# First norm's sums on VectorE, input first, and one weight tile behind every second modulation unit

## The reference, cut to what matters

```python
h = x + pos_embed_2d(rows, GRID_W, D)[None]          # latent tokens
hc = ctx                                             # context tokens
ml = (silu(c) @ w_ada + b_ada).reshape(B, 9, D)      # modulation, latent
mc = (silu(c_ctx) @ w_ada + b_ada).reshape(1, 9, D)  # modulation, context
u  = modulate(rmsnorm(h,  norm_g[0]), ml[:, 0], ml[:, 1])
uc = modulate(rmsnorm(hc, norm_g[0]), mc[:, 0], mc[:, 1])
h  = h  + 0.5 * ml[:, 2] * swiglu(u,  ffn_w_in[0], ffn_w_out[0])
hc = hc + 0.5 * mc[:, 2] * swiglu(uc, ffn_w_in[0], ffn_w_out[0])
```

## Time and profile before

| what | us |
|---|---|
| median of 3 runs | 2897.46 (2894.49 to 2897.83) |
| profiled execution | 2883.62 |
| its span, first to last instruction | 2881.8 |
| PE busy in it | 2823.4 (98%) |
| DVE busy | 1633.4 (57%) |
| ACT busy | 968.0 (34%) |
| POOL busy | 237.2 (8%) |

### The profile page before, as it was taken

The page is one execution under the profiler, slowest core; times in us unless marked ns, Lnnn a source line. Parts: engine busy times, 40 slices in busy tenths (PEclk is TensorE's granted clock), DMA queues, the critical chain, the costliest instruction groups (busy, mean ns, idle before and its releaser), DMA issues. The chain is left out here.

```text
span 2881.8 us, 47633 instructions
## 1 busy us (share of the span) xinstructions
PE 2823.4 (98%) x17840; PEld 2475.6 (86%) x17840; DVE 1633.4 (57%) x2197; ACT 968.0 (34%) x1443; POOL 237.2 (8%) x388
## 2 busy tenths in 40 slices
PE   5999999999999999999999999999999999999998
PEld 3688888888888888888888888878999999999998
DVE  2557677676776652223225666655675555555555
ACT  2222222222222221121214555544354444444444
POOL 3000000000000000000101013555120000000001
PEclk8999999999999999999999999999999999999999
DMA  9766676667888856555563566695556556566664
GB/s 361 282 215 209 203 225 202 220 214 232 316 303 317 296 198 203 195 191 165 193 194 105 164 183 194 197 271 167 157 176 193 188 188 189 182 189 189 189 189 147
DMA packets 410321, 604.42 MB, mean 210 GB/s; under 512 B 52960, under 2 KB 303840, under 8 KB 401520
## 3 DMA queue, kind: packets, MB, share of 16 engines
q1 hardware_dynamic: 361536, 417.42, 46.0%
q10 hardware_dynamic: 48688, 185.73, 19.4%
HBM read 560.02 MB, written 43.02 MB: 209 GB/s over the span
## 5 line engine op out<-in xcount | busy, mean ns | idle before, releaser
L1943 DVE TENSOR_TENSOR wl<-raw,wh 128x1024 fp32r<-128x1024 f32 x638 | 782.0, 1232 | 833.8 <-ACT wh L1467 832.0
L1467 ACT CAST wh<-raw 128x1024 fp32r<-128x1024 f32 x638 | 664.6, 1047 | 1466.9 <-PE ps L760 1426.0
L759 PE MATMUL ps<-xl,wh 128*128 128x512 f32 (+1 forms) x2560 | 968.8, 378 | 0.0
L758 PE MATMUL ps<-xh,wh 128*128 128x512 f32 (+1 forms) x1904 | 722.3, 379 | 3.2 <-DVE xl L1994 2.5
L760 PE MATMUL ps<-xh,wl 128*128 128x512 f32 (+1 forms) x1904 | 716.7, 376 | 0.0
L759 PEld LDWEIGHTS ps<-xl,wh 128*128 128x128 f32 x2560 | 481.9, 188 | 89.2
L758 PEld LDWEIGHTS ps<-xh,wh 128*128 128x128 f32 x1904 | 358.7, 188 | 77.7 <-issue 8.4
L760 PEld LDWEIGHTS ps<-xh,wl 128*128 128x128 f32 x1904 | 358.2, 188 | 65.9
L758 PE MATMUL ps<-x2h,wh 128*128 128x256 f32 x1408 | 394.8, 280 | 1.7 <-DVE x2l L1994 1.7
L759 PE MATMUL ps<-x2l,wh 128*128 128x256 f32 x1408 | 396.0, 281 | 0.0
L760 PE MATMUL ps<-x2h,wl 128*128 128x256 f32 x1408 | 394.6, 280 | 0.0
(11 more groups left out here) (274 smaller groups left out, 2665.9 us busy)
## 6 DMA issues: line engine op xcount, KB each, us to landing
raw<-in_ffn_w_in SPq DMA_DIRECT2D x704, 256.0 KB, 3.5
raw<-in_ffn_w_out SPq DMA_DIRECT2D x176, 512.0 KB, 4.5
abuf<-in_w_ada ACTq DMA_DIRECT2D x64, 1024.0 KB, 6.7
abuf<-in_w_ada ACTq DMA_DIRECT2D x96, 512.0 KB, 3.9
xl<-d_h ACTq DMA_DIRECT2D x80, 512.0 KB, 4.3
ada_t<-in_ada SPq DMA_DIRECT2D x64, 512.0 KB, 9.1
raw<-in_w_in SPq DMA_DIRECT2D x128, 256.0 KB, 3.5
raw<-in_w_out SPq DMA_DIRECT2D x32, 512.0 KB, 4.9
```

The source lines that it names most:

```text
L758: mm(out, ah, bh, start=first, stop=False, skip_group_check=reopened)
L759: mm(out, ah, bl, start=False, stop=False, skip_group_check=reopened)
L1467: nc.scalar.copy(wh[:, t % HL, :], raw[:, t % RAW, :]).then_inc(hi_done, 1)
L1943: tt(tl, raw[:, t % RAW, :], th.bitcast(F32), ALU.subtract).then_inc(lo_done, 1)
```

## The change

- SP requests the two halves of the latent input first, ahead of all of `w_ada` (they were issued by ACT, between its other loads). The context halves stay on ACT.
- SP requests a weight tile behind every second unit (i = 1, 3, ..., 15: tiles 0 to 7) instead of one behind each unit from i = 3 on (tiles 0 to 12).
- The position table and the 13 additions of squares move from POOL to DVE. POOL keeps the power -0.5.
- PE's `norm` stands in unit i = 2 (the third unit) instead of i = 4.
- PE works tile t behind unit 2t + 3: tiles 0 to 5 behind units 3, 5, 7, 9, 11, 13 instead of 6, 7, 8, 9, 11, 13.
- DVE norms one feature block per unit, and splits tile t behind unit 2t + 2, the unit just ahead of the tile's own. ACT rounds tile t behind blocks 2t and 2t + 1. Tiles 7 and 8 are split ahead of the last columns, tile 9 behind the last block.

```diff
-FIRST_TILES = {6: 0, 7: 1, 8: 2, 9: 3, 11: 4, 13: 5, 15: 6}
+FIRST_TILES = {2 * t + 3: t for t in range(K_TILES - 1)}
...
+            for b in range(2):
+                k = slice(8 * b, 8 * b + 8)
+                sp.dma_start(h_lat[:, k, :], xT[:, k, :]).then_inc(x_in[b], 16)
             for i in range(ADA_SS):
                 ada_load(i)
-                if i >= 3:
-                    up_load(0, 0, i - 3)
-            for x in range(ADA_SS - 3, UP_TILES):
+                if i % 2:
+                    up_load(0, 0, i // 2)
+            for x in range(K_TILES, UP_TILES):
                 up_load(0, 0, x)
...
-                    if i == 4:
+                    if i == 2:
                         norm(0, NTOK, 7)
...
-            for t in range(AHEAD):
+            for t in range(K_TILES - 1):
+                high(0, 2 * t)
+                high(0, 2 * t + 1)
                 split(0, 0, t)
...
+            def position(b):
+                rows, wide = SEQ // GRID_W, GRID_W
+                dve.wait_ge(x_in[b], 16)
...
+                tt(lat, lat, add.broadcast_to([P, 8, rows, wide]), ALU.add).then_inc(h_set, 1)
+
+            def add_squares(k):
+                dve.wait_ge(sq_done, squares_at(0, k))
+                if k == 1:
+                    i = tt(nacc[:], sq[:, 0, :], sq[:, 1, :], ALU.add)
+                else:
+                    dve.wait_ge(nacc_done, sums_at(0, k) - 1)
+                    i = tt(nacc[:], nacc[:], sq[:, k % 2, :], ALU.add)
+                i.then_inc(nacc_done, 1)
...
             start()
-            k = 0
-            for i in range(ADA_SS):
+            for b in range(2):
+                position(b)
+            for k in range(1, 10):
+                add_squares(k)
+            ada_row(0, 4)
+            for k in range(10, KT - 2):
+                add_squares(k)
+            first_columns(0)
+            ada_row(1, 5)
+            mean_square(0, NTOK, 7)
+            ada_row(2, 4)
+            first_columns(1)
+            dve.wait_ge(cols_set, 2)
+            for k in range(2):
+                scaled(0, k, 7)
+            for k in range(2):
+                low(0, k)
+            split(0, 0, 0)
+            for i in range(3, ADA_SS):
                 ada_row(i, 4 + i % 2)
-                if i:
-                    first_columns(i - 1)
-                if i == 3:
-                    for t in range(AHEAD):
-                        split(0, 0, t)
-                if i == 4:
-                    mean_square(0, NTOK, 7)
-                if i >= 5:
-                    dve.wait_ge(cols_set, i)
-                    now = range(k, min(2 * (i - 4), i))
-                    for k in now:
-                        scaled(0, k, 7)
-                    for k in now:
-                        low(0, k)
-                    k += 1
-                if i in FIRST_TILES:
-                    split(0, 0, FIRST_TILES[i] + AHEAD)
+                first_columns(i - 1)
+                dve.wait_ge(cols_set, i)
+                scaled(0, i - 1, 7)
+                low(0, i - 1)
+                if i % 2 == 0:
+                    split(0, 0, i // 2 - 1)
+            split(0, 0, K_TILES - 1)
+            split(0, 0, K_TILES)
             first_columns(ADA_SS - 1)
             dve.wait_ge(cols_set, ADA_SS)
-            for k in range(k, KT):
-                scaled(0, k, 7)
-                low(0, k)
+            scaled(0, KT - 1, 7)
+            low(0, KT - 1)
+            split(0, 0, K_TILES + 1)
             up_pairs(0, 0)
```

More of the change, by code:

```diff
@@ L1472, in start @@
                     k = slice(8 * b, 8 * b + 8)
-                    act.dma_start(h_lat[:, k, :], xT[:, k, :]).then_inc(x_in[b], 16)
                     act.dma_start(h_ctx[:, k, :], ctxT[:, k, :]).then_inc(x_in[2 + b], 16)
@@ L1518, in load_piece, with up_pairs @@
                     act.dma_start(abuf[:, i % 2].rearrange("p s n -> p (s n)"), src).then_inc(abuf_in[i % 2], 16)
-            def up_pairs(r, m, before=None):
+            def up_pairs(r, m):
                 for x in range(UP_TILES):
-                    if before is not None:
-                        before(x)
-                    split(r, UP_TILES, m * UP_TILES + x + AHEAD)
+                    if m or x >= K_TILES - 1:
+                        split(r, UP_TILES, m * UP_TILES + x + AHEAD)
                     if x < LOAD_AT and m:
@@ L1853, in _ @@
                 square(0, k, 2)
-            for t in range(AHEAD):
+            for t in range(K_TILES - 1):
+                high(0, 2 * t)
+                high(0, 2 * t + 1)
                 split(0, 0, t)
[L1857 to L1862, removed]
+            high(0, KT - 2)
+            split(0, 0, K_TILES - 1)
+            split(0, 0, K_TILES)
+            high(0, KT - 1)
+            split(0, 0, K_TILES + 1)
+            up_pairs(0, 0)
             with act.Fori(0, PIECE_BOTH - 1) as r:
@@ L1952, in start @@
                 dve.wait_ge(cpad_set, 3)
+            def position(b):
+                rows, wide = SEQ // GRID_W, GRID_W
+                dve.wait_ge(x_in[b], 16)
+                lat = h_lat[:, 8 * b:8 * b + 8, :].rearrange("p k (r c) -> p k r c", c=wide)
+                if b == 0:
+                    add = cols[:, C_POSR:C_POSC].rearrange("p (k r) -> p k r", r=rows).unsqueeze(3)
+                else:
+                    add = cols[:, C_POSC:C_IDENT].rearrange("p (k c) -> p k c", c=wide).unsqueeze(2)
+                tt(lat, lat, add.broadcast_to([P, 8, rows, wide]), ALU.add).then_inc(h_set, 1)
[3 more added lines that the diff above has]
+                    i = tt(nacc[:], sq[:, 0, :], sq[:, 1, :], ALU.add)
+                else:
+                    dve.wait_ge(nacc_done, sums_at(0, k) - 1)
+                    i = tt(nacc[:], nacc[:], sq[:, k % 2, :], ALU.add)
+                i.then_inc(nacc_done, 1)
             def ada_row(i, bank):
@@ L2516, in _ @@
             start()
-            k = 0
-            for i in range(ADA_SS):
-                ada_row(i, 4 + i % 2)
-                if i:
-                    first_columns(i - 1)
-                if i == 3:
-                    for t in range(AHEAD):
-                        split(0, 0, t)
-                if i == 4:
-                    mean_square(0, NTOK, 7)
-                if i >= 5:
-                    dve.wait_ge(cols_set, i)
-                    now = range(k, min(2 * (i - 4), i))
-                    for k in now:
-                        scaled(0, k, 7)
-                    for k in now:
-                        low(0, k)
-                    k += 1
-                if i in FIRST_TILES:
-                    split(0, 0, FIRST_TILES[i] + AHEAD)
+            for b in range(2):
[17 more added lines that the diff above has]
+            for i in range(3, ADA_SS):
+                ada_row(i, 4 + i % 2)
+                first_columns(i - 1)
[4 more added lines that the diff above has]
+                    split(0, 0, i // 2 - 1)
+            split(0, 0, K_TILES - 1)
+            split(0, 0, K_TILES)
             first_columns(ADA_SS - 1)
             dve.wait_ge(cols_set, ADA_SS)
-            for k in range(k, KT):
-                scaled(0, k, 7)
-                low(0, k)
+            scaled(0, KT - 1, 7)
+            low(0, KT - 1)
+            split(0, 0, K_TILES + 1)
             up_pairs(0, 0)
@@ L2722, in _ @@
             pool.wait_ge(half_set, 1)
[L2723 to L2733, removed]
+            pool.wait_ge(ms_done, 2)
+            rms(slice(0, NTOK // P))
             norm_streams()
```

## The result

The changed kernel takes 2901.39 us (median of 12 runs, 2890.45 to 2906.11) against 2894.54 us of the kernel before (12 runs, 2884.16 to 2897.83). The ratio is 1.0028, 95% interval 1.0015 to 1.0041: some 8 us slower, and clear of no change, since the interval leaves out 1. The forecast was 2 us faster.

What follows compares the result with a forecast made beforehand. PE bounds the kernel through the end of its first stage. The norm's 15.6 us gain, less 13.6 given back in waits for splits, leaves 2.0: 2897.46 - 2.0 = 2895.5 us, range 2882 to 2902.

Steps and rivals of the forecast that it cites:

- What bounds the kernel: Whole kernel: PE is busy from 137 us to 1000 us, so the time it gets through the first stage decides.
- all of a shift of the first stage reaches the end: Behind the first evacuation by ACT: whatever is gained or lost ahead of it is kept to the end.
- The norm earlier by 15.6: Norm behind the third unit: its spreading ends at 41.85 us instead of 57.45, 15.6 us earlier.
- The branch with the high level: PE at the norm: high clock shortens quarter, columns, sums and spreading by 3.0 us; gain 5.0, 2892.5 us; chance 20%.
- The work moved to DVE hidden: Position table and 13 additions on DVE, ahead of the norm: cost nothing, with a cover of 0.8 to 8.6 us.
- The new wait: Ahead of each tile: split ready 5.02 us behind the unit's copy, PE ready at 2.9, so PE waits some 2.1 us.
- The chain's 12.73 us per cycle: Tile loop: PE copy, DVE, ACT, DVE, PE set the cycle of two units and a tile, 5.02 + 7.71 us.
- The weight tiles requested later: SP's requests: five tiles fewer ahead of the last quarter, 6.5 us of DMA, taking nothing off PE.
- the step that a tile behind this wait takes 5.7 us: Tile loop: a tile was counted as 5.6 us of PE's own work, with the clock staying high.
- The third rival: Tile loop: the clock falls in seven waits of 2.1 us; 17 us slower, 2914.5 us; chance 8%.
- The rival's price of 19 for seven falls: Tile loop: each clock fall loses 2.8 us, 19 in all, less the gain of 2.0, so 17 slower.
- The chances: Whole kernel: faster by over 0.2% 27%, slower by over 0.2% 11%, within 62%; low clock at norm, chain-bound loop 59%.

Runs made afterwards that it cites:

- the filler of 16: The changed kernel with 16 useless matmuls on PE ahead of each of tiles 0 to 5; ratio 1.0088 to the kernel before.
- the last experiment: The changed kernel with each tile split one unit earlier and PE waiting for x block by block within a tile; ratio 0.9959 to the kernel before.
- the short filler: The changed kernel with 5 useless matmuls on PE ahead of each of tiles 0 to 5; ratio 0.9995 to the kernel before.
- mean first: The kernel before, with DVE splitting tiles 0, 1 and 2 behind the norm's mean instead of behind unit 3; ratio 0.9993 to the kernel before.
- split between scaled and low: The changed kernel, ACT rounding tile t behind block 2t (t > 0), DVE splitting it ahead of block 2t + 1's low part; ratio 0.9965 to the kernel before.

## Why the prediction was wrong

What bounds the kernel, and that all of a shift of the first stage reaches the end: right. Before and after agree behind the evacuation within 0.7 us.

The norm earlier by 15.6: right, 15.4. The quarters came as counted, and the level at the norm was the low one in this execution. The branch with the high level exists too, in two of the eight traces with the new order (the filler of 16 and the last experiment, from 37.27 and 37.21 us): there the spreading began 2.7 us earlier than in the changed kernel (3.0 was worked out).

The work moved to DVE hidden: right. The table took 2.29 a half and an addition 0.69, by the duration of single instructions, which is near the lower bound.

The new wait, 2.1 us per tile: right, 2.23 by its rows. The chain's 12.73 us per cycle: right where the clock stood, 12.74 in the experiment with the short filler and 12.75 with the input on ACT. That it fits to the hundredth is luck: in the trace with the short filler it was 5.10 us from the copy to the tile and not 5.02 (68.58 to 73.68), and 7.64 from the tile to the next copy and not 7.71 (60.94 to 68.58).

The weight tiles requested later cost nothing: right; PE waits for no quarter in the loop.

Wrong was the step that a tile behind this wait takes 5.7 us, that is, that the clock stays high through the new waits; it took 7.25 to 8.5. The third rival was what happened, and I gave it 8%. The ground I gave against it was that PE had stood still for 1.66 us at tile 0 of the kernel before, and the clock had stayed. That is one wait, and a shorter one than the new ones; nor does its length settle it, for the changed kernel's own tile 0 waited only 1.50 us, and its clock fell. Six cycles, from 47.08 to 135.63, took 88.55 us, and six of 12.73 are 76.4: 12.2 us lost there, 1.0 in the tail and 0.2 at the start. The rival's price of 19 for seven falls was too high, since the clock came back after some 3 to 6 us, so that a tile lost 1.5 (four times) or 2.8 (twice), and the tail 1.0; the sum of 17 slower was 12.2 in the span, and 8 by the ratio. The other traces show that the number of falls varies, which may be why the ratio says less than this trace.

The chances were wrong with it. The wait was a new one, the largest that PE has in this loop, with six repeats; and a clock that had fallen at 37 us, in a stop of 2.98 us ahead of the quarter at 39.14, was in the earlier trace rows. What stood against the fall deserved no more than an even chance.

## What to carry to other kernels

A wait of PE can cost more than its length, when the clock falls with it: here the waits cost 10.3 us at the end, and the lower clock that came with them 12.3 more. So before an order of work that puts a fresh 2 us wait ahead of each block of matmuls is priced, it should be looked at whether the operand can be made one unit earlier; here that was a matter of moving the split calls on DVE and ACT, and turned a ratio of 1.0028 into 0.9964. A look-ahead that seems idle in a trace (splits made three tiles ahead) may be what keeps a chain over three engines off the path.

## What the runs showed of the hardware

- Waits of 2.1 to 2.2 us ahead of a tile put the granted clock down in 15 of 20 cases, and left it in others of the same execution (cycles of 12.7 beside 14.3). Single waits of 0.94 and 0.86 us ahead of a tile never did. Between them it goes both ways at tile 0: 1.26 us (input on ACT) and 1.66 (the kernel before, and mean first) left it high, 1.50 (the changed kernel), 1.56 (sums on POOL) and 1.93 (split between scaled and low) didn't. And a row of short waits for quarters, none over 0.64 us, put it down once (mean first). So the length of the last wait doesn't decide alone; what does isn't shown.
- The level at the norm, with the same program ahead of it, was the low one in the changed kernel and the high one in the last experiment: 0.57 and 0.36 us for a pair of its matmuls.
- Matmuls of 32 columns that all went into one group of columns took 0.44 us each (7.09 / 16); four into four groups took 0.48 together (1.93 / 4).
- In the second network, at a granted clock of 1.00, PE did 1721 matmuls in 200 us in the profiled execution of the changed kernel and 1700 in that of the last experiment:

```profile
2400.00:2600.00 200.00, 200.00 (x1721) 1.00 0.60 188
```

```profile
2400.00:2600.00 200.00, 200.00 (x1700) 1.00 0.60 184
```

Over the second network, which takes some 750 us, 1.2% is an estimated 9 us, as much as the change moved by the ratio. Why they differ wasn't tried.
